# The last three weight units of two row projections, run for one half of the tokens and then for the other

## What is computed

```
def rmsnorm(x, g):
    return x * lax.rsqrt(jnp.mean(x * x, axis=-1, keepdims=True) + EPS) * g
...
# first block
x = x + rmsnorm(mix @ w_out, post_mix_g)                    # "wout"
h = rmsnorm(x, pre_ffn_g)                                   # norm before "up"
u = h @ w_up                                                # "up", 2048 -> 2 x 5632
...
x = x + rmsnorm((gelu(gate) * val) @ w_down, post_ffn_g)    # "down", 5632 -> 2048
...
# second block, first layer (16 meta tokens are added to the 256)
y = rmsnorm(h, pre_norm)
q, k, v, gate = split(y @ attn_w_in)                        # "aqk", then "av", "ag"
```

## Time and profile before

| | before |
|---|---|
| median of 3 executions | 2173.89 us (2173.82 to 2177.01) |
| the profiled execution | 2173.85 us, of which the span of the trace 2172.1 us |
| mean granted PE clock | 0.999 |
| PE busy | 2145.8 us, 99% of the span, 14559 matmuls |
| DVE busy | 1520.8 us, 70% |
| ACT busy | 1184.2 us, 55% |
| POOL busy | 220.5 us, 10% |
| HBM read | 396.32 MB, 184 GB/s over the span |

### The profile page before, as it was taken

The page is one execution under the profiler, slowest core; times in us unless marked ns, Lnnn a source line. Parts: engine busy times, 40 slices in busy tenths (PEclk is TensorE's granted clock), DMA queues, the critical chain, the costliest instruction groups (busy, mean ns, idle before and its releaser), DMA issues.

```text
span 2172.1 us, 38987 instructions
## 1 busy us (share of the span) xinstructions
PE 2145.8 (99%) x14559; PEld 1986.3 (91%) x14559; DVE 1520.8 (70%) x2091; ACT 1184.2 (55%) x1781; POOL 220.5 (10%) x146
## 2 busy tenths in 40 slices
PE   9999999999999999999999999999999999999998
PEld 8888899999889999999988889999999999999987
DVE  6676755668578888888855556999777565567755
ACT  5455654545455555555544446555655565676553
POOL 0000000000003223232300000221000000012110
PEclk9999999999999999999999999999999999999999
DMA  8655566657656565666666665566435647555454
GB/s 291 197 156 163 157 202 211 196 170 240 212 162 200 187 215 185 216 193 194 212 202 203 201 202 177 186 192 194 122 119 182 184 140 234 173 158 146 137 201 157
DMA packets 259012, 405.60 MB, mean 187 GB/s; under 512 B 16671, under 2 KB 115868, under 8 KB 257852
## 3 DMA queue, kind: packets, MB, share of 16 engines
q1 hardware_dynamic: 257204, 396.87, 58.6%
q10 hardware_dynamic: 1688, 7.07, 0.9%
HBM read 396.32 MB, written 4.22 MB: 184 GB/s over the span
## 4 chain that ended last, share of the span: by engine, by line
PE 91%; DVE 5%; ACT 3%; issue 1%; DMA 0%; DVEq 0%; ACTq 0%; SPq 0%
PE bank L2317 30%; PE bank L2313 23%; PE bank L2426 14%; PE bank L2310 12%; PE bank L2909 3%; PE bank L2332 2%; DVE wboth L1394 1%; ACT wboth L707 1%; PE bank L2656 1%; PE bank L2878 1%; PE bank L2834 1%; PE bank L2628 1%; DVE xtok L1548 0%; PE bank L2694 0%; PE bank L2361 0%
## 5 line engine op out<-in xcount | busy, mean ns | idle before, releaser
L1394 DVE TENSOR_TENSOR wboth<-raw,wboth 128x1024 fp32r<-128x1024 f32 (+1 forms) x748 | 909.2, 1229 | 514.7 <-ACT wboth L707 511.9
L707 ACT ACTIVATE wboth<-raw 128x1024 fp32r<-128x1024 f32 (+1 forms) x748 | 771.1, 1039 | 609.8 <-PE bank L2313 263.3
L2313 PE MATMUL bank<-aboth,wboth 128*128 128x512 f32 x2496 | 812.8, 382 | 2.3 <-DVE aboth L1613 1.1
L2310 PE MATMUL bank<-aboth,wboth 128*128 128x256 f32 x2496 | 658.8, 274 | 1.0 <-DVE wboth L1394 1.0
L2317 PE MATMUL bank<-aboth,wboth 128*128 128x272 f32 (+1 forms) x5184 | 624.1, 280 | 4.6 <-DVE aboth L1613 3.1
L2317 PEld LDWEIGHTS bank<-aboth,wboth 128*128 128x128 f32 x5184 | 606.1, 190 | 8.6 <-issue 4.0
L2313 PEld LDWEIGHTS bank<-aboth,wboth 128*128 128x128 f32 x2496 | 461.1, 189 | 60.4 <-issue 1.6
L2310 PEld LDWEIGHTS bank<-aboth,wboth 128*128 128x128 f32 x2496 | 478.2, 192 | 12.6 <-issue 2.7
L2426 PE MATMUL bank<-wboth,ghi 128*128 128x512 f32 x704 | 209.8, 379 | 0.9 <-DVE wboth L1394 0.9
L2937 POOL CAST ghi<-pr 128x256 f32 x44 | 84.4, 1918 | 691.1 <-DVE pr L1882 691.1
L2426 PEld LDWEIGHTS bank<-wboth,ghi 128*128 128x128 f32 x704 | 133.1, 189 | 20.2 <-DVE wboth L1394 1.3
(11 more groups left out here) (373 smaller groups left out, 1870.4 us busy)
## 6 DMA issues: line engine op xcount, KB each, us to landing
raw<-in_w_up SPq DMA_DIRECT2D x176, 512.0 KB, 4.6
raw<-in_w_in SPq DMA_DIRECT2D x156, 512.0 KB, 4.1
raw<-in_attn_w_in SPq DMA_DIRECT2D x96, 512.0 KB, 4.1
raw<-in_gla_w_in SPq DMA_DIRECT2D x96, 512.0 KB, 3.9
raw<-in_w_down SPq DMA_DIRECT2D x80, 512.0 KB, 4.6
raw<-in_w_out SPq DMA_DIRECT2D x32, 512.0 KB, 4.4
raw<-in_attn_w_out SPq DMA_DIRECT2D x32, 512.0 KB, 4.3
raw<-in_gla_w_out SPq DMA_DIRECT2D x32, 512.0 KB, 4.1
```

The lines of the kernel that those rows point to most:

```text
L707: act.activation(whi[:, u % RING, 0:c], raw[:, u % RAW, 0:c], ACT.Copy).then_inc(whi_ready, 1)
L1394: dve.tensor_tensor(wlo[:, u % RING, 0:c], raw[:, u % RAW, 0:c], whi[:, u % RING, 0:c].bitcast(F32), ALU.subtract).then_inc(wlo_ready, 1)
L2310: mm = pe.matmul(bank[:, base + t, 0:T], w[1][:, k, col:col + P], in_turns(rhs(0, k0 + k)), start=False, stop=False)
L2313: mm = pe.matmul(bank[:, base + t, 0:2 * T], w[0][:, k, col:col + P], parts_in_turns(both(k0 + k)), start=first, stop=last)
```

## The change

In the last trip of wout and of down, PE runs all units but the last three (`HELD_UNITS`) as before, then these three for tt = 0, then for tt = 1 (`rows_held`). ACT and DVE begin with the norm of half 0 when its rows are complete, and PE turns each half by itself (`turn_halves`), with fewer matmuls on constants. The splits for the second and third unit of the following stream are held in both places, since a slot comes free only with the second pass. In down the units with one k-tile stand at the start of each chunk and no longer at its end. `norm_by_halves` replaces `norm` behind down, with another order of pieces (`X_PIECES`).

```diff
@@ -323,7 +323,7 @@
             if ph == "oabc":
                 return (2 * (j % 2), 2) if j % 8 < 4 else (j % 8 - 4, 1)
             if ph == "down":
-                return (2 * (j % 24), 2) if j % 24 < 20 else (20 + j % 24, 1)
+                return (j % 24, 1) if j % 24 < 4 else (2 * (j % 24) - 4, 2)
             if ph == "up":
                 return 4 * (j % 8 // 2), 4
             if ph == "lr":
...
@@ -458,7 +458,8 @@
         OUT_STREAM = [None, "wout", "down", "aout"]
         N_XN = [0, None, 3, 11]
         X_PIECES = [None] + [((0, 0, 512), (1, 0, 512), (0, 512, 1024), (1, 512, 1024), (0, 1024, D), (1, 1024, D))] \
-            + [tuple((tt, 512 * c, 512 * c + 512) for c in (3, 0, 1, 2) for tt in range(2))] * 2
+            + [tuple((tt, 512 * c, 512 * c + 512) for c, tt in ((3, 0), (0, 0), (3, 1), (0, 1), (1, 0), (1, 1), (2, 0), (2, 1)))] \
+            + [tuple((tt, 512 * c, 512 * c + 512) for c in (3, 0, 1, 2) for tt in range(2))]
         N_XU = [None, 0, 6, 14]
         N_XS = [None, 2, 6, 20]
         N_XT = [None, None, 0, 14]
...
@@ -815,11 +816,24 @@
             def rows_out_of(b):
 
                 def read_out(i, chunk, u, n):
+                    if 2 * i + chunk == 3 and b < 3:
+                        return
                     for tt in range(2):
                         passed(u, 2 * tt + 2, i, n)
                         rows_squared(b, 2 * i + chunk, tt)
                 return read_out
 
+            def last_squared(b, tt):
+
+                passed(U0[OUT_STREAM[b]] + 2 * UNITS[OUT_STREAM[b]] - 1, (4 - 2 * HELD_UNITS, 4)[tt], 0, 0)
+                rows_squared(b, 3, tt)
+
+            def split_behind_held(b, n):
+
+                last = U0[OUT_STREAM[b]] + 2 * UNITS[OUT_STREAM[b]]
+                act.wait_ge(tile_pass, 4 * (last - HELD_UNITS) + 2 * (HELD_UNITS + n))
+                split(last + n)
+
             def y_mean(b, tt):
 
                 act.wait_ge(y_sum, 2 * (b - 1) + tt + 1)
...
@@ -847,10 +861,14 @@
 
             def norm_first(b):
 
+                last_squared(b, 0)
                 y_mean(b, 0)
+                split_behind_held(b, 1)
+                last_squared(b, 1)
                 y_mean(b, 1)
                 for g in range(2):
                     norm_hi(b, g)
+                split_behind_held(b, 2)
 
             def rows_spread():
 
...
@@ -908,12 +926,30 @@
                 x_normed(b, 5)
                 split(U0[ph] + LEAD - 1)
 
+            def norm_by_halves(b):
+
+                last_squared(b, 0)
+                y_mean(b, 0)
+                split_behind_held(b, 1)
+                tail_squared(b, 0)
+                last_squared(b, 1)
+                tail_mean(b, 0)
+                y_mean(b, 1)
+                x_normed(b, 1)
+                tail_squared(b, 1)
+                tail_mean(b, 1)
+                norm_hi(b, 0)
+                norm_hi(b, 1)
+                x_normed(b, 4)
+                x_normed(b, 5)
+                split_behind_held(b, 2)
+
             def later_hi(b):
 
                 def after(i, j):
                     if j < 2:
                         for tt in range(2):
-                            x_normed(b, (6, 0)[j] + tt)
+                            x_normed(b, (6, 0)[j] + (1, 2)[b == 2 and j == 1] * tt)
                     if j < 6:
                         norm_hi(b, 2 + j)
                 return after
...
@@ -1082,9 +1118,9 @@
             load_roots(2)
             down_rows = rows_out_of(2)
             trip("down", 0, down_rows, after=lambda i, j: rows_moments(2, 0) if j == 28 else None)
-            trip("down", 1, down_rows, after=lambda i, j: rows_moments(2, j // 24 + 1) if j in (4, 28) else None, held=1)
-
-            norm(2, "aqk")
+            trip("down", 1, down_rows, after=lambda i, j: rows_moments(2, j // 24 + 1) if j in (4, 28) else None, held=HELD_UNITS - 1)
+
+            norm_by_halves(2)
 
 
             def feature_out(dst, T, func, scale=1.0):
...
@@ -1557,18 +1593,24 @@
                 dve.tensor_scalar(rxdiag[:, tt * P:(tt + 1) * P], ident[:, :], xstat[:, 1, tt:tt + 1], None, ALU.mult)\
                    .then_inc(rx_diag, 1)
 
+            def split_behind_held(b, n):
+
+                split(U0[OUT_STREAM[b]] + 2 * UNITS[OUT_STREAM[b]] + n)
+
             def norm_first(b):
 
                 y_summed(b, 0)
                 y_inverse(b, 0)
                 x_piece(b, 0)
+                rows_gained(b, 3, 0)
+                split_behind_held(b, 1)
                 y_summed(b, 1)
                 y_inverse(b, 1)
                 x_piece(b, 1)
-                rows_gained(b, 3, 0)
                 norm_lo(b, 0)
                 norm_lo(b, 1)
                 rows_gained(b, 3, 1)
+                split_behind_held(b, 2)
                 x_piece(b, 2)
                 x_piece(b, 3)
 
...
@@ -1635,6 +1678,32 @@
                 norm_lo(b, 0)
                 norm_lo(b, 1)
                 split(U0[ph] + LEAD - 1)
+                x_piece(b, 6)
+                x_piece(b, 7)
+
+            def norm_by_halves(b):
+
+                rows_gained(b, 3, 0)
+                y_summed(b, 0)
+                y_inverse(b, 0)
+                x_piece(b, 0)
+                row_terms(b, 0)
+                x_piece(b, 1)
+                rows_gained(b, 3, 1)
+                y_summed(b, 1)
+                x_scale(b, 0)
+                y_inverse(b, 1)
+                x_piece(b, 2)
+                row_terms(b, 1)
+                x_piece(b, 3)
+                x_scale(b, 1)
+                x_normed(b, 3)
+                norm_lo(b, 0)
+                norm_lo(b, 1)
+                split_behind_held(b, 1)
+                x_piece(b, 4)
+                x_piece(b, 5)
+                split_behind_held(b, 2)
                 x_piece(b, 6)
                 x_piece(b, 7)
 
...
@@ -1895,8 +1964,8 @@
                     row_coefficients(2)
 
             trip("down", 0, down_rows, after=beside_down)
-            trip("down", 1, down_rows, after=beside_down, held=1)
-            norm(2, "aqk")
+            trip("down", 1, down_rows, after=beside_down, held=HELD_UNITS - 1)
+            norm_by_halves(2)
 
 
             def qk_norm(i, j):
...
@@ -2406,14 +2475,14 @@
                         mm = pe.transpose(bank[:, 4, k * TM:(k + 1) * TM], mrow[:, k * P:(k + 1) * P], ident[0:TM, 0:TM])
                     mm.then_inc(par_turned, 1)
 
-            def rows_of_unit(ph, b, i, j):
+            def rows_of_unit(ph, b, i, j, parts=(0, 1)):
 
                 u, _, begins, ends = unit_begin(ph, i, j)
                 c = 2 * i + chunk_of(ph, j)[0]
                 k0, nk = unit_tiles(ph, j)
                 w = [t[:, u % RING, :].rearrange("p (k n) -> p k n", k=2 if nk == 1 else nk) for t in (whi, wlo)]
                 src = (ahi, alo) if b == 1 else (ghi, glo)
-                for tt in range(2):
+                for tt in parts:
                     if begins and c < 2:
                         pe.wait_ge(acc_free, 4 * (C0[ph] - 2) + row_bank(b, c, tt) + 1)
                     elif begins:
...
@@ -2442,6 +2511,23 @@
 
                 for _ in range(n):
                     pe.matmul(bank[:, 0 if b == 3 else 7, 0:P], ones[:, :], ident[:, :], start=True, stop=True)
+
+            def rows_held(ph, b):
+
+                for tt in range(2):
+                    for j in range(UNITS[ph] - HELD_UNITS, UNITS[ph]):
+                        rows_of_unit(ph, b, 1, j, (tt,))
+
+            def turn_halves(b, src, half_ready, busy):
+
+                for tt in range(2):
+                    keep_busy(b, busy[tt])
+                    pe.wait_ge(*half_ready[tt])
+                    for g in range(2):
+                        for k in (2 * g, 2 * g + 1):
+                            mm = pe.transpose(turned(k)[:, tt * P:(tt + 1) * P], src[:, tt, k * P:(k + 1) * P], ident[:, :])
+                        if tt:
+                            mm.then_inc(xn_turned, 1)
 
             def norm(b):
 
...
@@ -2581,13 +2667,12 @@
                     branch = chunk_of("oabc", j)[0] % 3
                     features("oabc", i, j, lambda part, k: (yhi, ylo)[part][:, 4 * branch + k, :], TB)
             for i in range(TRIPS["wout"]):
-                for j in range(UNITS["wout"]):
+                for j in range(UNITS["wout"] - (0, HELD_UNITS)[i]):
                     rows_of_unit("wout", 1, i, j)
                     if (i, j) == (0, 10):
                         meta_mean(0)
-            keep_busy(1, 12)
-            for g in range(2):
-                norm_turn(1, g)
+            rows_held("wout", 1)
+            turn_halves(1, xtok, [(x_updated, N_XU[1] + 1), (x_updated, N_XU[1] + 2)], (0, 5))
 
             def spread_rows():
 
...
@@ -2610,9 +2695,10 @@
                 for j in range(UNITS["up"]):
                     features("up", i, j, model(TB), TB, both=model_parts)
             for i in range(TRIPS["down"]):
-                for j in range(UNITS["down"]):
```

(10 more changed lines are left out.)

1 line of the change is left out of this document (added).

## The result

The changed kernel takes 2180.36 us (median of 13 runs, 2179.65 to 2182.26), the kernel before, on the same chip, 2175.64 us (13 runs, 2173.82 to 2177.01). The ratio, which is estimated from all the runs and not from the two medians alone, is 1.0024, with a 95% interval of 1.0016 to 1.0031: slower, by more than the measurement is uncertain. The forecast was 2178.0, most likely no difference that could be told.

A forecast was written before the change was run, and what follows sets the result against it. The tensor engine, busy 99% of the span, was taken as the bound, so only its waits matter. Terms of 3.1, 1.1 and -0.1 us summed to 4.1 us on 2173.89, giving 2178.0 us, range 2175.6 to 2180.6.

The forecast's parts named there:

- rival 1: Start of down: PE's clock falls in the wait of about 4 us, costing 2 us more, 2180; chance 0.16.
- Term A: Start of down: with one-tile units first PE loses 4.17 us waiting for unit 3 instead of 1.08, +3.1 us.
- Term B: End of down: low part gains 1.94 us, aqk's third unit loses 3.01 us to the order behind it, +1.1 us.
- Term C: End of wout: the norm's 1.24 us gain is used up by the held split before two updates, -0.1 us.
- Rival 2: Heavier contention, GpSimd between the next splits: 3.7 us at down's start, 1.5 at its end, 2179; chance 0.14.
- Rivals 3 and 4: Start of down costs only 1 us, 2175.9, chance 0.13; or both norms keep their whole gain, 2170.7, chance 0.05.
- rival 4: Norms behind wout and down keep their whole gain, 1.94 + 1.24 us, start of down costs 0: 2170.7; chance 0.05.

The follow-up runs named there:

- the table alone: The kernel before with one line of the change, down's single-tile units at the start of each chunk: 2179.48 us, ratio 1.0023.
- the pieces ahead: The changed kernel with VectorE's updates of x pieces 4 and 5 behind down moved ahead of the four low parts: 2177.72 us, ratio 1.0016.
- the kernel with the wait filled: The changed kernel with 15 matmuls on constants on PE ahead of unit 3 of down: 2178.33 us, ratio 1.0020.
- the middle order: The changed kernel with the four single-tile units of each chunk of down at units 10 to 13: 2175.01 us, ratio 1.0005.
- the mended kernel: The changed kernel with single-tile units mid-chunk, pieces 4 and 5 updated before down's low parts, wout's second held split after pieces 2 and 3: 2172.07 us, ratio 0.9988.
- wout's split behind: The changed kernel with single-tile units mid-chunk and, behind wout, the second held split after the updates of pieces 2 and 3: 2175.01 us, ratio 1.0003.

## Why the prediction was wrong

**What failed** is the clock's term, which the forecast's sum put at nothing. It charged the wait of 4 us at the start of down with lost work only and left the clock to rival 1 with a chance of 0.16, "Against it: the wait is shorter than the observed one". The one observed was the end of the program, and a shorter wait was taken to be safe because nothing showed the opposite. The runs show that it isn't: the clock falls in or behind 3.93 us in every trace where the wait is empty (after, the table alone, the pieces ahead), and inside a wait of 2.63 us in one. It costs 1.64 to 2.6 us, where rival 1 said 2. None of the 13 runs of the kernel after is under 2179.65, and the kernel with the wait filled reached 2177.97, 1.7 us less. So very likely every one of them had the fall, though only one has a trace. The Trainium skill (TensorE: Matmul & The Clock Gate, "Why this matters for your kernels") has the rule that spoke for rival 1, no long idle gaps between bursts of matmuls; the trace of the kernel after agrees, 0.50 in the slices of 1097 to 1100.

With rival 1 as the likeliest case, the forecast would have been 2180 and slower.

A second step failed beside it. The 4.1 us of waits were read as "just inside" of what a measurement can tell, 4.3 us. The interval of the measured ratio reaches only 1.6 us to either side, and the kernel with the wait filled, which shows the waits without the fall at the start of down, has 1.0020 [1.0011, 1.0029]: the forecast's own sum can be told from nothing. Without the clock the change would have been slower too.

**Term A** was right, +3.1 against 3.06 measured with the clock held up. Unit 3 was forecast at 1095.65 and came at 1095.64. The loss was forecast at 4.17 us; the interval between the matmuls was 4.31 us, of which 0.22 is the normal one. DVE's half split took 1.02 us beside GpSimd's subtraction, from 1094.57, where alone it takes 0.69: this stretching was in the forecast. That no second wait stands behind unit 3 was right as well.

**Term B** was right in sum and in both parts: +1.1 against +1.13. The first low part was forecast at 6.1 us after the last matmul (6.17), the third unit's split 5.9 us behind it (5.91), the third unit 10.66 us behind it (10.67), and the experiment with the pieces ahead shows that DVE's order makes the loss. One detail differs: PE's wait of 1.3 us before the third group of transposes isn't there, since the clock was low at 1329 to 1332 and aqk's first unit took 4.69 instead of 3.02 us. That cost nothing: with the middle order the same unit took 3.02 us, PE waited 1.34 us behind it, and the third unit came after 17.20 us all the same.

**Term C** was right, -0.1 against -0.13, and so was its cause: with the split out of the way the transposes came 1.13 us earlier (bound: -1.2). It could keep only 0.69 us of that.

**Rival 2**, more contention, did not come: A measured 3.06 us, not 3.7. **Rivals 3 and 4** did not either. Three further edits (units in the middle, pieces ahead, split behind) brought the part of rival 4 that lies in the norms, 2.3 us in all where it had 3.2.

**The runs of the kernel before** beside the kernel after reached from 2173.82 to 2177.01 us, with a median of 2175.64, higher than beside the experiments (2174.13 and 2174.36). Against the latter the kernel after is 6 us slower, as its trace says. What set these runs apart is open. Falls of the clock in the norms are a possible cause: in the traces of other kernels one cost from nothing to 1.1 us, but the one trace of the kernel before has none there.

## What to carry over

An empty wait of the tensor engine has two prices: the work not done, and the matmuls behind it at half the rate. Here 4 us of idle cost 1.6 to 2.6 us on top, a wait of 2.6 us paid it in one trace and, by the times, in part of the executions, one of 1.3 us in none. So a lengthened wait is to be counted with both prices, and filled if it can't be removed. When units change size, count the work that is left ahead of the first unit whose preparation starts at a fixed time: every half-size unit there lengthens the wait by what it lacks. And an update that others wait for goes ahead of a split that was merely held back; that order, together with the one-tile units in the middle, turned the same change from 0.24% slower to 0.12% faster.

## What was not expected of the hardware

- The clock can fall after PE has resumed (at 1096.8, 1.2 us behind the first matmul) or inside the wait (in the slice of 1094 to 1096), for the same wait of 3.93 us. What decides between them no run here shows.
- Norms whose stalls are filled but for gaps of 0.5 to 1.3 us still show falls in part of the executions: at 621 to 624.5 us with constant matmuls in the wait and in the mended kernel, not in the kernel after; at 1763.1 to 1766.5 in the one with wout's split behind, with the same gaps of 0.8 and 1.1 us as in the kernel after, which had none there. What such a fall costs depends on the wait behind it. At down's end it cost nothing in the kernel after, where PE had to wait anyway, and 1.1 us with the pieces ahead. At wout's end it delayed the start of down by 0.2 us in the order of the kernel after and by 0.85 us in the mended kernel, and at 1763 it cost 0.8 us. That is more than some of the edits are worth.
